# Fourth block of the first MLP group as a Strassen block, squared values of the other three in SBUF

## The reference

```python
def sq_relu_mlp(h, w1, w2):
    return jnp.square(jax.nn.relu(h @ w1)) @ w2
...
        h = rmsnorm(x, norm_mlp[l])
        x = x + sq_relu_mlp(h, mlp_w1[l], mlp_w2[l])
```

## Time and profile before

| | |
|---|---|
| median of 3 runs | 1959.07 us |
| profiled execution, device time | 1958.74 us |
| its span | 1956.9 us |
| PE busy, 12723 matmuls | 1934.6 us, 99% |
| PE weight loads | 1643.2 us, 84% |
| DVE | 1251.6 us, 64% |
| ACT | 967.0 us, 49% |
| POOL | 1134.0 us, 58% |
| mean granted PE clock | 0.998 |

### The profile page before, as it was taken

One profiled execution on the slowest core, in us unless ns is written; L12 is line 12 of the kernel. 1 busy time (PEld: TensorE's weight loads), 2 busy tenths in 40 slices (PEclk: granted clock), 3 DMA queues, 4 the chain that ended last, 5 costly groups with the idle time before them and its releaser, 6 DMA issues.

```text
span 1956.9 us, 33326 instructions
## 1 busy us (share of the span) xinstructions
PE 1934.6 (99%) x12723; PEld 1643.2 (84%) x12723; DVE 1251.6 (64%) x1914; ACT 967.0 (49%) x1664; POOL 1134.0 (58%) x1356
## 2 busy tenths in 40 slices
PE   7999999999999999999999999999999999999998
PEld 6788788888888889998887887888898888989987
DVE  5887778856145756767358787787631566676662
ACT  6754555345445644344455546353553655444344
POOL 5564554956834555666564555467576446556653
PEclk9999999999999999999999999999999999999999
DMA  6323333333422333333342233333343233333331
GB/s 188 111 77 81 82 82 93 87 107 106 149 82 81 96 101 101 99 103 97 101 100 77 74 85 84 79 87 87 118 135 114 71 97 95 100 102 100 100 103 70
DMA packets 197275, 190.89 MB, mean 98 GB/s; under 512 B 23738, under 2 KB 190204, under 8 KB 196732
## 3 DMA queue, kind: packets, MB, share of 16 engines
q1 hardware_dynamic: 196252, 186.66, 32.9%
q10 hardware_dynamic: 864, 2.10, 0.3%
HBM read 184.51 MB, written 3.15 MB: 96 GB/s over the span
## 4 chain that ended last, share of the span: by engine, by line
PE 92%; DVE 4%; ACT 2%; issue 1%; DMA 0%; DVEq 0%; POOL 0%; SPq 0%; ACTq 0%
PE gemm L685 72%; PE mix L685 19%; DVE h_lo L1946 1%; DVE work L1937 1%; DVE work_split L1946 1%; DVE x_t L1937 0%; PE mix L1267 0%; DVE work L1946 0%; DVE sums_raw L1937 0%; DMA work<-in_norm_mix_dram 0%; DVE gate_t L1946 0%; ACT work_split L1570 0%; ACT work L1577 0%; DVE mix L1937 0%; PE mix L1162 0%
## 5 line engine op out<-in xcount | busy, mean ns | idle before, releaser
L678 POOL TENSOR_TENSOR w_lo<-w_raw,w_hi 128x256 fp32r<-128x256 f32 x676 | 587.5, 869 | 794.7 <-ACT w_hi L1401 794.7
L679 POOL TENSOR_TENSOR w_lo<-w_raw,w_hi 128x256 fp32r<-128x256 f32 x676 | 597.0, 883 | 0.0
L685 PE MATMUL gemm<-h_hi,w_hi 128*128 128x512 f32 x1312 | 519.2, 396 | 2.3 <-DVE h_lo L1946 2.3
L685 PE MATMUL gemm<-h_hi,w_lo 128*128 128x512 f32 x1312 | 511.1, 390 | 0.0
L685 PE MATMUL gemm<-h_lo,w_hi 128*128 128x512 f32 x1312 | 511.1, 390 | 0.0
L685 PE MATMUL gemm<-work_split,w_hi 128*128 128x512 f32 (+1 forms) x1552 | 447.1, 373 | 0.3
L1401 ACT ACTIVATE w_hi<-w_raw 128x512 fp32r<-128x512 f32 x676 | 378.9, 621 | 52.5 <-DMA w_raw<-in_w_in_dram 22.6
L685 PEld LDWEIGHTS gemm<-work_split,w_hi 128*128 128x128 f32 x1552 | 281.5, 188 | 51.1 <-DVE work_split L1946 1.1
L685 PEld LDWEIGHTS gemm<-h_hi,w_hi 128*128 128x128 f32 x1312 | 246.3, 188 | 62.8 <-issue 6.6
L685 PEld LDWEIGHTS gemm<-h_hi,w_lo 128*128 128x128 f32 x1312 | 246.3, 188 | 51.9
L685 PE MATMUL gemm<-work_split,w_lo 128*128 128x512 f32 (+1 forms) x776 | 288.4, 372 | 0.0
(11 more groups left out here) (363 smaller groups left out, 2688.0 us busy)
## 6 DMA issues: line engine op xcount, KB each, us to landing
w_raw<-in_mlp_w_dram SPq DMA_DIRECT2D x256, 256.0 KB, 2.7
w_raw<-in_w_in_dram SPq DMA_DIRECT2D x208, 256.0 KB, 2.7
w_raw<-in_xattn_w_kv_dram SPq DMA_DIRECT2D x64, 256.0 KB, 3.0
w_raw<-in_w_branch_dram SPq DMA_DIRECT2D x32, 256.0 KB, 2.7
w_raw<-in_w_out_dram SPq DMA_DIRECT2D x32, 256.0 KB, 2.7
w_raw<-in_xattn_w_q_dram SPq DMA_DIRECT2D x32, 256.0 KB, 2.9
w_raw<-in_xattn_w_o_dram SPq DMA_DIRECT2D x32, 256.0 KB, 2.7
w_raw<-in_w_in_dram SPq DMA_DIRECT2D x32, 128.0 KB, 3.3
```

Source lines behind the costliest of these rows:

```text
L678: pool.tensor_tensor(lo[:, 0:half], raw[:, 0:half], hi[:, 0:half].bitcast(F32), ALU.subtract)
L679: pool.tensor_tensor(lo[:, half:], raw[:, half:], hi[:, half:].bitcast(F32), ALU.subtract).then_inc(split_ready, 1)
L685: return pe.matmul(o, w, a, start=start, stop=stop, skip_group_check=True)
```

## The change

up0_3 becomes the first block with sums. PE runs `up_sums(0, 3)` in place of the plain block; the counts of sums go from 24 to 26 per layer, and the list SUM_STEPS begins with (0, 3), with no down block ahead of it. DVE makes the two pairs of weight sums of up0_3 between output(2) and low(3), and the sums of up1_0 come in the step of (0, 3), by the same loop as all others. Outputs 6 and 7 go; `products_out(0, 3)` and two `hidden_low` take their place. ACT's `feed` of up0_3 now waits for the sums and copies them. UPX[1] moves from the PSUM bank M[0] to `gate_t`'s second row in SBUF, since the block now needs M[0]. SP and POOL have the same instructions in the same order.

```diff
-    return 16 * (int(name[2]) - 1) + 4 * int(name[4]) + part if name.startswith("up") and name[2] != "0" else None
+    step = 4 * (int(name[2]) - 1) + int(name[4]) + 1 if name.startswith("up") else -1
+    return 4 * step + part if step >= 0 else None
...
-        UPX = [TH[:, 0, :], M[0]]
+        UPX = [TH[:, 0, :], TH[:, 1, :]]
...
-        SUM_STEPS = [(q, c) for q in range(1, 4) for c in range(4)]
+        SUM_STEPS = [(0, 3)] + [(q, c) for q in range(1, 4) for c in range(4)]
...
-                for c in range(4):
+                for c in range(3):
                     gemm(f"up0_{c}", *H, ready=h_ready if c == 0 else None, ready_at=16)
...
-                        if (q, c) == (1, 0) and j == 0:
+                        if (q, c) == (0, 3) and j == 0:
                             pe.wait_ge(*of_layer(at["mm_turned_ready"], 12))
...
                 for q, c in SUM_STEPS:
-                    down(q - 1, c)
+                    if q:
+                        down(q - 1, c)
                     up_sums(q, c)
...
                 feed(first_unit("up0_3") + 4)
                 squared(3)
+                squared(4)
                 feed(first_unit("down0_0") + 2)
-                squared(4)
+                squared(5)
                 feed(first_unit("down0_0") + 4)
-                squared(5)
-                feed(sums0 + 2)
-                squared(6)
-                squared(7)
-                feed(sums0 + 8)
-                n = 8
+                n = 6
                 for t, (q, c) in enumerate(SUM_STEPS):
...
-                ahead = first_unit("up1_0")
+                ahead = first_unit("up0_3")
...
                 output(2)
+                weight_sums(ahead)
                 low(2)
+                sums_low(ahead)
                 output(3)
+                weight_sums(ahead + 2)
                 low(3)
+                sums_low(ahead + 2)
                 output(4)
                 low(4)
                 output(5)
-                weight_sums(ahead)
                 low(5)
-                output(6)
-                sums_low(ahead)
-                low(6)
-                output(7)
-                weight_sums(ahead + 2)
-                low(7)
-                sums_low(ahead + 2)
                 for t, (q, c) in enumerate(SUM_STEPS):
-                    residual(f"down{q - 1}_{c}")
-                    ahead = first_unit("up{}_{}".format(*SUM_STEPS[t + 1])) if t < 11 else None
+                    if q:
+                        residual(f"down{q - 1}_{c}")
+                    ahead = first_unit("up{}_{}".format(*SUM_STEPS[t + 1])) if t < 12 else None
```

More of the change, by code:

```diff
@@ L201 @@
     s5_val_ready=2, mghi_ready=8, attn_mm_turned_hi=12, sq_ready=24, attn_kqv_hi=20, attn_kt_ready=8, attn_q_ready=8, attn_vm_ready=4,
-    attn_p_exp=16, attn_pt_hi=8, attn_pt_ready=8, attn_ohi_ready=8, up_relu=20, up_hi=32, hx_ready=12, h_ready=24, weight_sums=24, sums_split=24, hg_decay_ready=5,
+    attn_p_exp=16, attn_pt_hi=8, attn_pt_ready=8, attn_ohi_ready=8, up_relu=19, up_hi=32, hx_ready=12, h_ready=24, weight_sums=26, sums_split=26, hg_decay_ready=5,
     th_used=38, hg_diff=13, s5_prm=1, hg_picked=8, hg_x=6, hg_kdecay_ready=1, hg_state_ready=2, y_act=8, y_ready=8,
@@ L1877, in squared @@
                     do(act.activation(MHID[0][0][:, n, :], UPX[1], ACT.Copy), uphi)
-                sums0 = first_unit("up1_0")
                 feed_past("up0_0")
@@ L1888, in _ @@
                 squared(3)
+                squared(4)
                 feed(first_unit("down0_0") + 2)
-                squared(4)
+                squared(5)
                 feed(first_unit("down0_0") + 4)
-                squared(5)
-                feed(sums0 + 2)
-                squared(6)
-                squared(7)
-                feed(sums0 + 8)
-                n = 8
+                n = 6
                 for t, (q, c) in enumerate(SUM_STEPS):
-                    ahead = first_unit("up{}_{}".format(*SUM_STEPS[t + 1])) if t < 11 else first_unit("down3_0")
-                    if t < 11:
+                    ahead = first_unit("up{}_{}".format(*SUM_STEPS[t + 1])) if t < 12 else first_unit("down3_0")
+                    if t < 12:
                         feed(ahead + 2)
@@ L1910, in _ @@
                         n += 1
-                    feed(ahead + (8 if t < 11 else 4))
+                    feed(ahead + (8 if t < 12 else 4))
                 squares(3, "norm_mix" if L < DEPTH - 1 else "norm_final")
@@ L2685, in products_out @@
                     dve.wait_ge(gemm_done[s], 2 * used + 2)
-                    dve.wait_ge(*of_layer(up_a, 8 + 4 * (q - 1) + c + 1))
+                    dve.wait_ge(*of_layer(up_a, 6 + SUM_STEPS.index((q, c)) + 1))
                     tt(both, first, M[0][:, SECOND], ALU.add)
```

## The result

| | before | after |
|---|---|---|
| median (range, runs) | 1959.24 us (1958.71 to 1959.58, 4) | 1981.29 us (1979.34 to 1981.8, 4) |
| ratio | | 1.0112, 95% from 1.0099 to 1.0124 |
| profiled execution, its span | 1958.74 us, 1956.9 us | 1980.88 us, 1979.1 us |
| mean granted PE clock | 0.998 | 0.995 |

The change costs 22.0 us. The forecast was 1976.5 with a range up to 1983: the sign, the places and most of the size came as worked out, and 4.5 us of the 22.0 were not in its sum.

The account below looks back on a forecast made before the run. PE, busy 99% of the span, was taken as the bound. Losses of 9.1 and 8.4 us in the two layers, saving inside, sum to 17.5; 1958.74 + 17.5 = 1976.2, plus 0.33 for the median: 1976.5 us, range 1968 to 1983.

Parts of the forecast that it names:

- The saving: On PE, up0_3 goes from 10.91 to 10.07 us: 0.84 us per layer, 1.7 us in all.
- The first wait: PE waits in front of up0_3 for about 1.4 us, released by POOL at 676.5.
- The second wait: PE waits between up0_3's second and third unit, 4.3 us (3.6 in the second layer), released by DVE's sums_lo.
- The last wait: PE waits about 5 us in down0_0's last quarter, released by DVE's work_split; last low part at 703.9 (703.2).
- the clock falls in a wait: Rival 3: PE's clock drops to half in its waits, 4 to 8 us more, about 1982; chance 0.12.
- the nine last matmuls: After the last low part, PE has 9 of down0_0's 48 matmuls left, taken as 2.04 us.
- 9.1: First layer's forecast loss in us, saving inside: down0_0 ends at 706.0 against 696.94.
- 8.4: Second layer's forecast loss in us, saving inside: down0_0 ends at 705.3 against 696.94, in first-layer times.
- Hidden after all (1): Rival: the added work ahead of up0_3 fits DVE's idle time and the saving stands, 1957.4 us; chance 0.09.
- Only the front wait (2): Rival: only waiting ahead of up0_3 costs, 4.8 and 4.0 us, hidden tiles in time, 1967.9 us; chance 0.09.
- Slower by less (4): Rival: a smaller loss, because overlaps were counted twice, 1960 to 1968 us; chance 0.06.
- the slack: In the old pattern, down0_0's last tile came 7.66 us behind the up block, needed at 8.86: 1.2 us.

Follow-up runs that it names:

- e4_sq3: The changed kernel with ACT's squared(3) moved ahead of the second pair of up0_3's units: 1975.34 us, ratio 1.008.
- e5_copy: The changed kernel with ACT copying the first product ahead of the sums and splits of up1_0's first pair: 1975.37 us, ratio 1.0082.
- e1_fill: The changed kernel plus unused matmuls on PE, 12 ahead of up0_3's third unit and 10 ahead of down0_0's last quarter: 1978.79 us, ratio 1.0099.
- the second pair of runs: `e6_order` and `e10_orderfill`, the same order without and with unused matmuls on PE: 1972.29 and 1969.99 us.
- e7_best: `e6_order` plus the order of `e5_copy` and further moves on DVE and ACT, with up1_0's first sums ahead of output(5): 1961.22 us, ratio 1.0013.
- e3_nosums: The changed kernel without up0_3's weight sums and ACT's copies of them, PE multiplying plain weight slices instead: 1961.58 us, ratio 1.0011.
- e6_order: The changed kernel with up0_3's weight sums earlier on DVE and ACT, and no PE wait for output(3) ahead of up0_3: 1972.29 us, ratio 1.0072.
- e8_both: The changed kernel with the moves of both `e4_sq3` and `e5_copy` on ACT: 1970.79 us, ratio 1.0059.
- e10_orderfill: `e6_order` plus 14 unused matmuls on PE ahead of down0_0's last quarter: 1969.99 us, ratio 1.0053.
- e2_sbuf: The kernel before with only the squared values moved from PSUM to SBUF: 1959.11 us, ratio 1.000.

## Why the prediction was right, and where it was off

**The saving.** 0.84 us per layer, right and never to be seen by itself. The reason given, that a loss would show and a gain could not, held.

**The first wait.** Forecast 1.4 us, released by POOL at 676.5; measured 1.58 and 1.60, with PE's start at 676.68. POOL had its unit done at 676.38 (the second half started at 674.94 and took 1.44), so the sum was right for POOL, but the block also waits for the `gemm` bank that output(3) empties, at 676.52. I had put output(3) at 676.7 and had not seen that PE waits for it. The two come within 0.2 us of each other, so it cost nothing in the forecast.

**The second wait.** The forecast's `sums_lo` ended at 685.8 (685.1 in the second layer), the measured one at 684.08 + 1.36 = 685.44. The wait was forecast as 4.3 and 3.6 us; the rows show 3.64 and 2.89 (with the later start of the block and the end of the matmuls ahead, which overlaps the wait by some 0.2 us, it is the same date). Low(3) took 0.92 (0.9 taken). The reason, squared(3) behind the copy of sums in ACT's queue, is what `e4_sq3` took away, for 6.0 us.

**The last wait.** products_out was forecast for 697.1 and started at 697.50; the last low part for 703.9 (703.2), and ended at 703.64 + 0.69 = 704.33, and at 1675.40, which is 703.06 in the first layer's times. So a chain through three engines, built from the old rows, was right to 0.4 us. Some of that is luck, since single steps were off by as much and in both directions: `sums_lo` ended 0.4 us early and low(4) took 0.69 (0.9 taken), but low(5) took 1.30 in the first layer (0.9 taken; 0.69 in the second) and the weight sums of up1_0 3.5 (3.3). `e5_copy` shows the other half: that ACT copies the first product last costs 5.9 us, some 3 of them by the clock.

**The clock: the step that failed.** The prediction held "the clock falls in a wait" as a rival to the forecast, with 0.12 for itself, and with its 4 to 8 us more. It is no rival. It comes with the waits that the forecast has, and its term belonged in the same sum. Its time of about 1982 lies within 1 us of the result, but by a larger clock term (4 to 8 us) than the one measured; the smaller terms below make up the difference. By dates it cost 3.0 us at the last quarter (`e1_fill`), 2.5 by the medians; 2.3 in the second pair of runs. The low clock behind the second wait (686.4 to 689.8) cost nothing at the end, since up0_3 is waited for by no one before ACT's product copy at 697.00: it delays PE only in a stretch in which DVE is later still. The Trainium skill, "TensorE: Matmul & The Clock Gate", section "Part 1: The HAM clock gate", says that activity releases the half clock; here 3.2 us of work behind the first layer's last wait and 5.7 behind the second's ran at 0.50 before it came back, and that is why a wait of 2.4 us costs more than itself.

**The rest of the 4.5 us.** The prediction gave the nine last matmuls 2.04 us from the last low part on; at full clock they take 2.34 (`e1_fill`), 0.3 more per layer. With the 0.43 on DVE and the clock that is 9.1 + 0.43 + 0.3 + 1.2 = 11.0 in the first layer (measured 10.95), and 8.4 - 0.14 + 0.3 + 1.9 = 10.5 in the second (20.69, less the 10.31 by which down3_0 of the first was late, is 10.4). Between up1_0 and down3_0 of the first layer 0.6 us were given back: before, up2_2 started 0.47 us behind its place (a wait for `sums_lo`, 0.34 in its row), and after it does not. This isn't the change either, since `e1_fill`, with the same order, has the wait again (915.3 us from up1_0 to the fixed place in the second layer, as before; 914.6 in after). That leaves 21.1 us at the last down blocks, and the profiled spans differ by 22.2: the last stores took 4.2 us from issue to landing in the execution of after and 3.1 in that of before. `e1_fill`, with the same work at the end, doesn't have this 1.1. I put it down to what differs from one execution to the next (after's four runs lie within 2.5 us), but no run here settles it.

**The rivals.** Hidden after all (1): fell; even `e7_best`, which hides nearly all of the sums in front, has the two waits of 0.7 and 0.6 us at the end. Only the front wait (2): fell, but its point of decision, products_out no later than 2.0 us behind the block, was borne out by `e3_nosums`: 3.5 us, 1.5 too many, gave 1.1 us of wait per layer. Slower by less (4): fell.

## What to carry to other kernels

A block that gets cheaper on the engine that sets the end saves little, while what feeds it may stand in the middle of full queues: work out when each queue comes to the new work, and compare that with the slack (1.2 us here, where the best order has 7.5 us more of DVE work in 31). If the reordering is needed to get even, look at the busy share in the stretch first: with DVE at 27 of 31 us, none of the orders that I ran gains. And a wait that is forecast for PE can carry a price of its own in clock, to be added to the sum and not set against it: here 2.3 to 2.5 us for two waits of 2.4 to 3.9 us.

## What the runs showed of the hardware that I had not expected

- The length of a wait alone doesn't tell whether the granted clock falls. It fell with waits of 2.40, 3.29 and 3.64 us after, of 2.72 in both layers of `e4_sq3` and of 3.90 and 3.79 in `e6_order`. It did not fall with 2.89 after, nor with 1.67 and 0.50 in `e5_copy`'s second layer. But in `e8_both`, behind 1.12 and 0.50 us of the first layer, it was 0.78 from 699 to 703, and it stayed up with the same waits in the second. Once down, it stayed at 0.50 for 3.4 us (703.5 to 706.9 after) to 6.8 us (1672.9 to 1679.7), mostly while PE was working again. Matmuls without use in the wait kept it at 1.00 there in `e1_fill` and `e10_orderfill`.
- Two SBUF sources beside POOL: a low part of 128 x 512 took 0.69 us alone and 0.92 to 1.30 beside POOL, a weight sum of 128 x 256 0.43 and 0.84, of 128 x 128 0.29 and 0.71. Which of the two engines loses can change from run to run: low(5) took 1.30 after, starting at 690.35 beside a POOL split of 0.74 (690.37), and 0.69 in `e1_fill`, starting at 690.58 beside a split of 1.27 (690.61). Moving all squares to SBUF still cost nothing in the old order (`e2_sbuf`).
